# Expert down products in three passes on split halves, in a fused two-block transformer kernel

## The reference, cut to what matters

```python
def expert_block(args):
    xb, e = args
    return (jax.nn.silu(xb @ w1[e]) * (xb @ w3[e])) @ w2[e]

ys = lax.map(expert_block, (xs, blk_expert)).reshape(P, D) * slot_w[:, None]
out = jax.ops.segment_sum(ys, slot_tok, num_segments=N + 1)[:N]
```

## Time and profile before

| | |
|---|---|
| median of 3 runs | 3241.24 us (3236.5 to 3248.06) |
| profiled execution, its own time | 3237.79 us |
| span of the profiled execution | 3236.2 us |
| mean granted TensorE clock | 0.978 of full speed |
| TensorE busy | 3033.9 us, 94% of the span |
| VectorE busy | 1716.0 us, 53% |
| ScalarE busy | 1269.9 us, 39% |
| GpSimd busy | 1094.5 us, 34% |
| DMA, mean over the span | 154 GB/s |

### The profile page before, as it was taken

The page is one execution under the profiler, slowest core; times in us unless marked ns, Lnnn a source line. Parts: engine busy times, 40 slices in busy tenths (PEclk is TensorE's granted clock), DMA queues, the critical chain, the costliest instruction groups (busy, mean ns, idle before and its releaser), DMA issues.

```text
span 3236.2 us, 36830 instructions
## 1 busy us (share of the span) xinstructions
PE 3033.9 (94%) x13878; PEld 2283.3 (71%) x13878; DVE 1716.0 (53%) x2829; ACT 1269.9 (39%) x1901; POOL 1094.5 (34%) x538
## 2 busy tenths in 40 slices
PE   5999999999989999999998999989999986999996
PEld 2666777888756677788885777877777854667664
DVE  5687663212258868322214654647774156666664
ACT  4454434223345453422324444223343223455552
POOL 1242344444324324444443554434444411000001
PEclk9999999999999999999998999999999998999998
DMA  5112563433321146374332335444342315999993
GB/s 223 57 55 72 178 201 114 141 123 103 96 85 59 59 143 221 122 288 137 97 111 77 121 114 176 122 123 115 114 111 72 120 30 201 352 376 385 390 387 126
DMA packets 192665, 501.25 MB, mean 155 GB/s; under 512 B 20144, under 2 KB 102192, under 8 KB 176384
## 3 DMA queue, kind: packets, MB, share of 16 engines
q1 hardware_dynamic: 168816, 415.15, 37.8%
q0 software_dynamic: 13200, 49.32, 4.0%
q10 hardware_dynamic: 10496, 34.71, 3.2%
HBM read 463.83 MB, written 35.29 MB: 154 GB/s over the span
## 4 chain that ended last, share of the span: by engine, by line
PE 75%; DVE 13%; DMA 4%; ACT 4%; issue 3%; ACTq 1%; POOL 1%; DVEq 0%; SPq 0%; POOLq 0%
PE banks L710 19%; PE banks L711 18%; PE banks L712 18%; PE banks L1348 4%; PE banks L1328 2%; PE banks L1330 2%; PE banks L1329 2%; DMA ring<-in_w_all 2%; PE banks L803 1%; PE banks L824 1%; PE banks L770 1%; PE banks L813 1%; DVE abuf L2193 1%; ACT w_hi L1461 1%; DMA routed<-arena 1%
## 5 line engine op out<-in xcount | busy, mean ns | idle before, releaser
L2838 POOL TENSOR_TENSOR w_lo<-ring,w_hi 128x1024 fp32r<-128x1024 f32 (+1 forms) x379 | 917.9, 2424 | 1393.4 <-ACT w_hi L1461 1393.3
L711 PE MATMUL banks<-h_lo,w_hi 128*128 128x512 f32 x2104 | 830.1, 395 | 0.0
L710 PE MATMUL banks<-hx_hi,w_hi 128*128 128x512 f32 (+2 forms) x1400 | 593.7, 424 | 29.8 <-DVE h_lo L2054 9.8
L1461 ACT ACTIVATE w_hi<-ring 128x1024 fp32r<-128x1024 f32 (+1 forms) x379 | 392.8, 1038 | 568.1 <-DMA ring<-in_w_all 481.4
L712 PE MATMUL banks<-hx_hi,w_lo 128*128 128x512 f32 (+2 forms) x1400 | 555.4, 397 | 0.0
L711 PEld LDWEIGHTS banks<-h_lo,w_hi 128*128 128x128 f32 x2104 | 400.4, 190 | 87.0 <-issue 10.4
L710 PEld LDWEIGHTS banks<-hx_hi,w_hi 128*128 128x128 f32 (+2 forms) x1400 | 267.8, 191 | 145.6 <-issue 74.6
L712 PEld LDWEIGHTS banks<-hx_hi,w_lo 128*128 128x128 f32 (+2 forms) x1400 | 267.3, 191 | 60.9 <-issue 0.2
L710 PE MATMUL banks<-hf_hi,w_hi 128*128 128x512 f32 x704 | 275.1, 391 | 4.0 <-DVE h_lo L2054 4.0
L712 PE MATMUL banks<-hf_hi,w_lo 128*128 128x512 f32 x704 | 274.4, 390 | 0.0
L2362 DVE TENSOR_TENSOR arena<-sgs,banks 128x512 f32<-128x512 f32 x44 | 30.3, 689 | 327.3 <-PE banks L712 327.3
(11 more groups left out here) (421 smaller groups left out, 5355.2 us busy)
## 6 DMA issues: line engine op xcount, KB each, us to landing
ring<-in_w_all SPq DMA_DIRECT2D x356, 512.0 KB, 3.8
arena<-in_w_all SPq DMA_DIRECT2D x26, 2048.0 KB, 11.5
arena<-in_w_all SPq DMA_DIRECT2D x96, 512.0 KB, 4.8
ring<-in_w_all SPq DMA_DIRECT2D x46, 1024.0 KB, 6.3
arena<-in_w_all SPq DMA_DIRECT2D x25, 1024.0 KB, 8.1
h<-in_w_all SPq DMA_DIRECT2D x23, 1024.0 KB, 7.9
abuf<-in_w_all SPq DMA_DIRECT2D x32, 512.0 KB, 5.2
routed<-abuf POOLq DMA_DIRECT2D x1, 12288.0 KB, 52.1
```

What stands on the lines that cost most here:

```text
L710: pe.matmul(bank[0:m, :], upper, hi, start=first, stop=False)
L711: pe.matmul(bank[0:m, :], upper, lo, start=False, stop=False)
L1461: act.activation(w_hi[s][:, 0:n], raw_w[s][:, 0:n], ACT.Copy).then_inc(w_upper, 1)
L2838: pool.tensor_tensor(w_lo[s][:, 0:n], raw_w[s][:, 0:n], w_hi[s][:, 0:n], ALU.subtract)\
```

## The change

The down products of blocks 1 to 21 are made in three passes on halves, as gate and up are; blocks 0 and 22 keep the float32 product, now called `down_whole`. ScalarE makes the upper halves of the down weights (`upper_down`, 4 instructions) into the place of `htok`, and of the hidden rows (`upper_hidden`, 1 instruction). GpSimd makes the lower halves of the down weights in place (`lower_down`, 4 subtractions), between its load of rows and its store. VectorE's copy of the hidden rows becomes a subtraction (`lower_hidden`). Some semaphores are merged elsewhere (`tiles_read` into `mod_summed`, `a_done` into `fd_act`, `cd_done` and `te_diff` into `te_exp` and `acs_tok_done`), with the counts that are waited for moved up accordingly.

```diff
+        hidb_hi, hidb_lo = halves("hidb_hi", "abuf", 6 * SEQ, SEQ), halves("hidb_lo", "sgs", SEQ, SEQ)
+        down_lo = [halves("down_lo0", "arena", shared_end + 2 * KC * SEQ, 4 * D), halves("down_lo1", "arena", 0, 4 * D)]
+        down_hi = halves("down_hi", "arena", shared_end + KC * SEQ, 4 * D)
...
             def down_block(b, par):
+                pe.wait_ge(sem("hidden_in"), b + 1)
+                pe.wait_ge(sem("ya_done"), b + 1)
+                pe.wait_ge(sem("yd2_done"), b + 1)
+                for k in range(4):
+                    pe.wait_ge(sem("down_lower"), 4 * b + (k - 3))
+                    for half in range(2):
+                        at = slice(k * D + half * SEQ, k * D + (half + 1) * SEQ)
+                        rows_hi, rows_lo = hidb_hi[:, k * P:(k + 1) * P], hidb_lo[:, k * P:(k + 1) * P]
+                        pe.matmul(sc_b[half], rows_hi, down_hi[:, at], start=(k == 0), stop=False)
+                        pe.matmul(sc_b[half], rows_hi, down_lo[par][:, at], start=False, stop=False)
+                        mm = pe.matmul(sc_b[half], rows_lo, down_hi[:, at], start=False, stop=(k == 3))
+                mm.then_inc(sem("d_done"), 1)
+
+            def down_whole(b, par):
                 pe.wait_ge(sem("wd_in%d" % par), 8 * (b - par) + 16)
...
+            def upper_down(b, par):
+                act.wait_ge(sem("wd_in%d" % par), 8 * (b - par) + 16)
+                act.wait_ge(sem("d_done"), b + 1)
+                for k in range(4):
+                    cols = slice(k * D, (k + 1) * D)
+                    act.activation(down_hi[:, cols], down[par][:, cols], ACT.Copy).then_inc(sem("down_upper"), 1)
+
+            def upper_hidden(b):
+                act.wait_ge(sem("hidden_turned"), b + 1)
+                act.activation(hidb_hi, aux, ACT.Copy).then_inc(sem("hidden_upper"), 1)
...
+            act.wait_ge(sem("scattered"), 2 * QT * 16)
+
+            def step(b, par, first=False, split=True):
+                if split:
+                    upper_down(b - 1, 1 - par)
                 act.wait_ge(sem("hidden"), b)
                 gate_half(b)
                 upper_weights(b + 1, (0, 1))
                 upper_rows(b + 1)
                 upper_weights(b + 1, (2, 3))
                 made_half(b - 1, 1 - par, first)
+                upper_hidden(b)
...
+            def lower_hidden(b):
+                dve.wait_ge(sem("hidden_upper"), b)
+                TT(hidb_lo, aux, hidb_hi, SUB).then_inc(sem("hidden_in"), 1)
...
+            def lower_down(b, par):
+                for k in range(4):
+                    cols = slice(k * D, (k + 1) * D)
+                    pool.wait_ge(sem("down_upper"), 4 * b + (k - 3))
+                    pool.tensor_tensor(down_lo[par][:, cols], down[par][:, cols], down_hi[:, cols], ALU.subtract)\
+                        .then_inc(sem("down_lower"), 1)
...
             with pool.Fori(0, (N_BLK - 1) // 2 - 1) as i:
                 for n in range(2):
-                    b = 2 * i + (n + 1)
+                    b = 2 * i + (n + 2)
                     pool.wait_ge(sem("rows_turned"), b + 1)
-                    load_rows(b + 2, 1 - n)
-                    store_made(b - 1, n)
...
+                    load_rows(b + 2, n)
+                    lower_down(b - 1, 1 - n)
+                    store_made(b - 1, 1 - n)
+            lower_down(N_BLK - 2, 1)
```

More of the change, by code:

```diff
@@ L1359, in _ @@
             turn_hidden(0)
-            down_block(0, 0)
+            down_whole(0, 0)
             rows_in(1, 1)
@@ L1376, in _ @@
                     turn_hidden(b)
-            down_block(N_BLK - 1, 0)
+            down_whole(N_BLK - 1, 0)
             keep_going(12)
@@ L1560, in _ @@
                     upper_to(2)
-                    act.wait_ge(sem("tiles_read"), 1)
+                    act.wait_ge(sem("mod_summed"), 1)
                 act.dma_start(relb, rel[ds(layer * (P * 8 * SEQ), P * 8 * SEQ)]
@@ L1692, in _ @@
                     if t == 1:
-                        act.wait_ge(sem("mod_summed"), layer + 1)
+                        act.wait_ge(sem("mod_summed"), layer + 2)
                         act.dma_start(csil, cond[:, ds(layer * D + D, D)]).then_inc(sem("c_in"), 16)
@@ L1750, in _ @@
             p = at("fd", "lin")
-            act.activation(gain[0:32, 0:1], v2("a_log")[0:32], ACT.Exp).then_inc(sem("a_done"), 1)
+            act.activation(gain[0:32, 0:1], v2("a_log")[0:32], ACT.Exp).then_inc(sem("fd_act"), 1)
             act.wait_ge(sem("f_bias"), 16)
@@ L1766, in _ @@
             summed(act, at("fd", "aux") + 2)
-            act.activation(cd_tok.rearrange("p a b -> p (a b)"), aux[:, 0:QT * 32], ACT.Exp).then_inc(sem("cd_done"), 1)
-            act.wait_ge(sem("te_diff"), 1)
+            act.activation(cd_tok.rearrange("p a b -> p (a b)"), aux[:, 0:QT * 32], ACT.Exp).then_inc(sem("te_exp"), 1)
+            act.wait_ge(sem("acs_tok_done"), 2)
             act.activation(te_tok, te_tok, ACT.Exp).then_inc(sem("te_exp"), 1)
@@ L1971, in _ @@
             upper_weights(1, (2, 3))
-            def step(b, par, first=False):
+            act.wait_ge(sem("scattered"), 2 * QT * 16)
+            def step(b, par, first=False, split=True):
+                if split:
+                    upper_down(b - 1, 1 - par)
                 act.wait_ge(sem("hidden"), b)
@@ L1979, in step @@
                 made_half(b - 1, 1 - par, first)
+                upper_hidden(b)
             for b in (1, 2):
-                step(b, b % 2, True)
+                step(b, b % 2, True, b == 2)
             with act.Fori(1, (N_BLK - 1) // 2 - 1) as i:
@@ L1986, in _ @@
             step(N_BLK - 2, 1)
+            upper_down(N_BLK - 2, 1)
             act.wait_ge(sem("hidden"), N_BLK - 1)
@@ L2164, in _ @@
             dve.wait_ge(sem("last_in"), 16)
-            modulate(ada_first[:, 14 * D:16 * D], 14, 2, sem("tiles_read"))
+            modulate(ada_first[:, 14 * D:16 * D], 14, 2, sem("mod_summed"))
             for layer in range(LAYERS):
@@ L2395, in _ @@
             mine(TS(pts[0][DR, :], raw[0][DR, :], 0.0, None, MAX))
-            dve.wait_ge(sem("fd_act"), 1)
+            dve.wait_ge(sem("fd_act"), 2)
             mine(TT(pr[0][FR, :], pr[0][FR, :], sm[0][FR, :], ADD))
@@ L2399, in _ @@
             mine(TT(dtT[DR, :], pts[0][DR, :], sm[0][DR, :], ADD))
-            dve.wait_ge(sem("a_done"), 1)
             mine(TS(pts[0][DR, :], dtT[DR, :], gain[DR, 0:1], -1.0, MUL, MUL))
@@ L2409, in _ @@
             dve.sem_inc(sem("acs_tok_done"), 1)
-            dve.wait_ge(sem("cd_done"), 1)
+            dve.wait_ge(sem("te_exp"), 1)
             TT(te_tok, aux[:, 0:QT * 32].rearrange("p (a b) -> p a b", b=32), acs_tok, SUB).then_inc(aux_free, 1)
             read(dve, a + 2)
-            dve.sem_inc(sem("te_diff"), 1)
-            dve.wait_ge(sem("te_exp"), 1)
+            dve.sem_inc(sem("acs_tok_done"), 1)
+            dve.wait_ge(sem("te_exp"), 2)
             mine(TT(te_tok, te_tok, dt_tok, MUL))
@@ L2791, in block_step @@
                 made_half(b - 1, 1 - par, first)
-                hidden_turned(b)
+                lower_hidden(b)
             for b in (1, 2):
@@ L2934, in _ @@
             load_rows(2, 0)
+            pool.wait_ge(sem("rows_turned"), 2)
+            load_rows(3, 1)
+            store_made(0, 0)
             with pool.Fori(0, (N_BLK - 1) // 2 - 1) as i:
                 for n in range(2):
-                    b = 2 * i + (n + 1)
+                    b = 2 * i + (n + 2)
                     pool.wait_ge(sem("rows_turned"), b + 1)
-                    load_rows(b + 2, 1 - n)
-                    store_made(b - 1, n)
-            pool.wait_ge(sem("rows_turned"), N_BLK - 1)
-            load_rows(N_BLK, 1)
-            store_made(N_BLK - 3, 0)
+                    load_rows(b + 2, n)
+                    lower_down(b - 1, 1 - n)
+                    store_made(b - 1, 1 - n)
+            lower_down(N_BLK - 2, 1)
             pool.wait_ge(sem("made_out"), (N_BLK - 2) * 16)
```

## The result

After the change the kernel takes 3306.54 us, the median of 4 runs (3303.71 to 3308.61), against 3242.47 us (3236.5 to 3248.06, 4 runs) before in the same session: a ratio of 1.0211, 95% interval 1.0193 to 1.023. That is 64 us slower, in the predicted range of 3256 to 3318 and 18.5 us above the predicted 3288. The profiled execution took 3307.34 us.

The account below looks back on a forecast made before the run. TensorE sets the pace at 19.10 us a block, DMA close behind; with the change, VectorE's and GpSimd's excluding reads add up to 22.1 us. 3237.8 + 54 - 2.5 - 1.4 = 3288 us, range 3256 to 3318.

Parts of the forecast that it names:

- the exclusion: VectorE and GpSimd in the expert blocks: they take turns, neither advancing while the other reads two operands from SBUF.
- The ring: From one down-product copy to the next, VectorE's and GpSimd's times add: 22.1 us a block in place of 19.10.
- each handing over hides some start-up: Turns between GpSimd and VectorE save 0.27 us a round, up to 0.8 for three; 0.5 us was taken off.
- How many blocks: Both engines' subtractions meet from the turn of block 4 to that of block 21: 18 x 3.0 = 54 us.
- late slots: Twice a late slot 1 stands on the chain; with spare time in each block these 2.5 us vanish.
- The range: Whole kernel, for 8 in 10: 3256 to 3318 us, from the likeliest case and the first half of the clock's.
- The likeliest case: The two engines' times add in each block: 3288 us, own range 3259 to 3301 us; chance 0.80.
- falling clock: Rival: TensorE idles 4.4 us a block, its clock halves, up to 36 us more, 3288 to 3324 us; chance 0.10.
- What would show it: Profile signs: VectorE's slot subtractions over 1.22 us mean, GpSimd's over 2.4 us, slot 0 requests 21 to 22.6 us apart.
- TensorE's gain: The down product as 24 short passes instead of 8 float32 matmuls: 1.37 us less for each of 21 blocks.
- side by side: Rival: GpSimd and VectorE subtract together without excluding each other, 18.7 us a block, 3209 to 3230 us; chance 0.05.
- At nothing: ScalarE's extra casts (4.6 us a block), down weights' arrival, SP's queue, merged semaphores and DMA bytes cost no time.

Follow-up runs that it names:

- run 1: Kernel before plus four GpSimd subtractions on the idle `htok` in each block, GpSimd waiting after each, nobody using the results; 3256.3 us, ratio 1.0049.
- run 2: Kernel before plus ten GpSimd memsets of 128 x 1024 in each block, which write SBUF and read nothing; 3235.24 us, ratio 0.999.
- run 8: Kernel before plus the same four GpSimd subtractions as run 1, but GpSimd waits only behind the fourth; 3271.18 us, ratio 1.0099.
- run 5: Changed kernel with GpSimd waiting for each of its four subtractions to be written before starting the next; 3291.51 us, ratio 1.0164.
- run 6: Run 4 with the next block's turned rows taken ahead of slot 1 on ScalarE and VectorE; 3210.23 us, ratio 0.9907.
- run 7: Changed kernel with GpSimd's subtractions left out, nobody making the down weights' lower halves, the middle pass rereading the upper; 3233.11 us, ratio 0.999.
- run 9: Changed kernel, GpSimd's four subtractions kept, with the next block's rows taken ahead of slot 1; 3308.22 us, ratio 1.0225.
- run 4: Changed kernel with VectorE making the down weights' lower halves ahead of slot 0, GpSimd only issuing transfers; 3238.59 us, ratio 1.0007.
- run 11: Run 6 with the last two of the four down subtractions on GpSimd, after waiting for VectorE's two; 3229.26 us, ratio 0.9974.

## Why the prediction was right, step by step

**What bounds the kernel, and the exclusion.** Right. TensorE alone set the 19.10 us, and rows 6 and 7, from other layers, foretold the contention. Runs 1, 2 and 8 show it by itself, run 2 that it needs reads. By the Trainium skill (SBUF — State Buffer, Who interferes with whom) a VectorE instruction with two SBUF inputs contends with a GpSimd instruction that reads SBUF, not with one that only writes. Runs 1 and 2 agree, 1.0049 and 0.999.

**The ring.** Right in kind, 0.9 us short in size: 22.1 us forecast, 23.04 measured, 0.4 above the upper bound of 22.6. Term by term, forecast and measured: VectorE's slots 9.08 and 9.08; GpSimd's four 9.6 and 9.47; copy to store 1.44 and 1.43; store to the first subtraction 1.16 and 1.20; rows 1.28 and 1.20. Two steps failed. "GpSimd starts with the first, so its fourth ends amid VectorE's slots 0 and 1", and "each handing over hides some start-up", for which I took 0.5 us off: in the steady blocks VectorE comes in only once, behind the fourth, and the timeline shows 0.13 us of start-up hidden. The 0.27 us for a round was itself too much. I had taken 0.69 and 2.40 us for the parts, but seven of VectorE's behind each other take 4.30 us, 0.60 from one to the next, and GpSimd's four 9.47, 2.36 from one to the next: 2 x 2.36 + 2 x 0.60 = 5.92 against 5.64 leaves 0.14 for a round. And the gated product, 0.60 us, was left out of the ring; had turns been taken it would have run beside GpSimd, as in run 5. The unrounded forecast was 22.06; with 0.60 for the gated product and 0.37 for the handing over, less 0.18 for the other terms together, it is 22.85, the block of the timeline. With GpSimd's 0.31 us more in every second block the mean is 22.99, which is that of VectorE's copies.

**How many blocks.** I took 18 x 3.0 = 54 us, less 3.9 got back. The count was right: 18 blocks, from the request for block 4 to that for block 22, make 69.9 us; the 17 later ones make 64.5, which is 17 x 3.94 = 67 less the 2.5 of the late slots. That the late slots vanish was right too. The forecast had 51.5 for the 18, so its error comes from the block time. (The medians are 64 us apart and the profiled executions 69.6, since the one before is 4.7 us under its median.)

**The range.** It held by its margin, not by the mechanism. The likeliest case had a range of its own, 3259 to 3301 us, and 3306.5 lies above it. What took it in, up to 3318, was room for a falling clock; the clock did fall and cost nothing that can be measured, as shown below. That part was luck.

**What would show it.** "VectorE's slot subtractions should have a mean over 1.22 us": 2.29 for slots 0 and 1. "Many near 2 to 3.5 us" is wrong, the median is 1.21 and one in a block takes up to 8.5; "GpSimd's new ones more than 2.4 us, some 3.5" is wrong, they never passed 2.41. Both figures are those of run 5, with 3.09 and 3.17. ("Never" holds from 2820 to 3120 us; in the first block the third and fourth took 3.37 and 3.36 by turns.) I had read the rows at 2457 and at 1593 us both as taking turns. At 2457 they did, VectorE's 2.86 us and GpSimd's two in 5.64; at 1593 the last four of VectorE's seven went behind each other and GpSimd stood 2.7 us. The steady blocks went like the second, with the sides exchanged; I had it only as "a VectorE that keeps them for a pair moves a wait".

**TensorE's gain.** The 1.4 us a block is real, run 6. My forecast took none of it inside the ring, rightly. But the "side by side" rival, 18.7 us a block and 3209 to 3230 us, would have been wrong even without contention: run 7 has 19.18. It left out that TensorE, once shorter, waits for the rows.

**At nothing.** Right. ScalarE's wait for the down weights is 2.0 us a block, but it is off the path: in the page's group of the new GpSimd subtractions the idle time before all 84 of them is 0.7 us.

```profile
L2968 POOL TENSOR_TENSOR down_lo<-arena,down_hi 128x1024 fp32r<-128x1024 f32 x84 | 200.5, 2419 | 0.7 <-ACT down_hi L1978 0.3
```

The casts are there when GpSimd's issues are over, as forecast.

**The clock.** Half of that rival came true. I had TensorE idle "in pieces between GpSimd's subtractions"; but its 24 passes of the down product run from 3006.35 to 3012.07 us without a wait, and over 400 us it waits for GpSimd three times, 2.5 us at most in all. It idles in one piece, for the rows. After the 2.9 us of idling the granted clock falls; in the timeline of TensorE in after:

```profile
3016.10 0.49 PE L1331 MATMUL banks<-slot_hi,xT_hi 128*128 128x512 f32 x1 [2.89 <-DVE xT_lo L2785]
...
3017.66 0.63 PE L1331 MATMUL banks<-slot_hi,xT_hi 128*128 128x512 f32 x1
3018.08 0.63 PE L1332 MATMUL banks<-slot_lo,xT_hi 128*128 128x512 f32 x1
```

Seven passes are 0.43 us apart in place of 0.23, 1.4 us. The granted clock from 3017.5 to 3020.8 us is 0.50, the lower level of 1.2 GHz, and 0.90 over the stretch of 50 us. It costs nothing that can be measured: in run 9 the rows are early, the clock is 0.95 to 1.00 in its four stretches, and the time is the same. TensorE wasn't in the ring.

## What to carry to other kernels

Before moving a two-input operation from VectorE to GpSimd, look whether VectorE has two-input operations on SBUF in the same stretch: if so, the times add, GpSimd's being twice as long, and VectorE may be the better place even at 94% busy (runs 4, 6, 11). Where both must read, look at the longest of VectorE's subtractions and not only at the median: in the change, run 8 and run 9 GpSimd's four held it to the last, and a wait between each two let it in (run 5 against the change, run 1 against run 8, 0.5% each). Run 11 had turns without such a wait, so measure before adding one. And when an engine that set the pace gets shorter, look for what it waits for next before counting the gain: here one line's order, the rows ahead of slot 1, was the difference between no gain (runs 4 and 7) and all of it (run 6).

## What the runs showed of the hardware that was not expected

- GpSimd can keep the shared reads over a whole run of instructions: VectorE's one subtraction then took up to 8.5 us in the change, up to 7.7 in run 8 and 10.94 in run 9. With up to 0.16 us of waiting between them, VectorE came in each time (run 5). But it came in as well in all 20 blocks of run 11, between two subtractions of GpSimd without a gap; the next one being ready is not what decides, and what does is open. By the Trainium skill (SBUF — State Buffer, SBUF: two separate sides) the holder has them for its one instruction and whoever starts first gets them; run 9 has VectorE starting first by the trace, 0.21 us, and waiting for all four. The measurement decides, and run 11 agrees with the page; whether the recorded start is the moment at which the engine asks for its operands, no run here shows.
- GpSimd's subtraction of 128 x 1024 took 1.89 us with one tile as both inputs and 2.37 to 2.41 with two. Which property of the operands makes the 0.5 us was not tried.
- Ten GpSimd `memset`s in each block, 29.86 us busy of 50 with its issues, left VectorE's subtractions at 1.22 us.
